# Eight of twelve modulation parts move from the start of a decoder layer into its projection stage

## The chip, the cores and the metric

The kernel runs on one core of one Trainium2 chip. The metric is device time in microseconds (us) of one execution of the whole layer; lower is better. The engines named below are PE (matrix multiply; PEld is its weight load), DVE (vector), ACT (scalar), POOL and SP. SP only issues DMA transfers here, and ACT issues a few small ones at the start.

## The reference, cut to what matters

```python
cond = silu(c)                                   # 1 x 1024
mod = cond @ ada_w[l] + ada_b[l]                 # 1024 x 6144 weights
shift1, scale1, gate1, shift2, scale2, gate2 = split(mod, 6)
h = rms_norm(x, norm_mix_w) * (1 + scale1) + shift1
mix = hybrid_mixer(h, ...)       # h @ w_in, RWKV-7, latent attention, gates, w_out
x = x + gate1 * mix
h = rms_norm(x, norm_ffn_w) * (1 + scale2) + shift2
x = x + gate2 * moe_ffn(h, ...)  # top 4 of 32 experts
```

All data are float32, with 512 tokens and 1024 features. `mod` is a single row of 6144 numbers. Of it the mixer's input needs only shift1 and scale1, which are the first 2048. The other 4096 are first used where the mixer's output is added to x.

## The kernel before

The kernel is a sequence of stages. Each is a block in which every engine has a program of its own, and engines wait for one another through counters (`wait_ge`, `then_inc`). A block ends when all engines have ended theirs.

**`phase_adaln`** makes all of `mod`. The 1024 x 6144 matrix comes as 12 chunks of 512 columns (2 MB each) through `g.ring`, which has three slots, on SP's queue. A chunk has eight groups of 128 rows. PE multiplies the first four (`PE_K`) with the condition repeated over its columns (`k{j}`, L319). DVE multiplies the other four by the condition and sums them (`accumulate`, L269), and PE adds that sum over the partitions with a matrix of ones (`p{j}`, L322). ACT copies the result (`mod{j}`, L240). A float32 matmul is two instructions in the trace. When the first four parts are there, PE turns them into columns (`mcol`, L328) and turns the normalised x (`xn`, L244) into feature-major form (`h{k}`, L336), and DVE applies scale and shift (L281) to give `hT`. Behind part 11 SP stores the other 4096 numbers in `mod_rows`.

**`phase_project`** multiplies `hT` by `w_in`. A feature block is eight matmuls (L454). The order of the first ten is l0, l1, r0 to r3, k0 to k3. ACT copies each out (`raw`, L494), and DVE mixes each with its shifted self (`shift`, L550 and L552). Behind k3 come the small products zw, za, g and ss. ACT makes sigmoids of zw and za (L506, L508) and later roots of ss (L517), while PE goes on with v and m. From the roots on DVE works through four long groups of elementwise steps (L573 to L603) and ends with L606. **`phase_rwkv`** is the recurrence.

**`phase_mla`** is the attention. Its last part goes over 32 units, eight heads for each of four blocks of 128 queries. For unit u PE issues `scores(u + 2)` (L1035, L1036), `turn(u)` (L1044) and `values(u - 1)` (L1053). DVE scales an output (L1206), takes a maximum (L1216), negates it (L1218) and inverts a sum (L1210). ACT makes the exponentials. At the start of this stage SP loads the three chunks OA, OB and GA. **`phase_output`** uses OA, OB and then GA, and reads `mod_rows` back over all partitions near its end. Routing and experts follow.

What sets the order is the hand-written program of each engine. The SP program matters most, because a wait in it also holds every transfer behind it.

## Time and profile before

| | us |
|---|---|
| median of 3 runs (1943.92 to 1948.35) | 1947.18 |
| the profiled execution | 1953.72 |
| its span in the profile | 1951.9 |
| lengths of the stages in that span: `phase_adaln` | 89.1 |
| first ten feature blocks of `phase_project` | 68.9 |
| rest of `phase_project` | 65.1 |
| the 32 units of attention, with the turn of their output | 58.2 |

Times of rows are us from the span's start. "Busy" is the time in which an engine has an instruction under way. The busy time of PE is modelled and includes its pipeline, so the distance between the starts of two PE rows says more than the length of one. "PEclk" is the granted TensorE clock as a share of full speed (1.00 is 2.4 GHz, 0.50 is 1.2 GHz).

### The profile page before, as it was taken

The numbers are of one execution on the slowest core, as the hardware profiler recorded it, in microseconds if no ns is written. First come the engines' busy times: TensorE is split into PE (matmuls) and PEld (weight loads), VectorE is DVE, ScalarE is ACT, GpSimd is POOL, SyncE is SP. The second block draws the span as 40 slices with busy tenths as digits, with TensorE's granted clock in tenths as the row PEclk, the third lists the DMA queues.
The fourth block names the chain that finished last, engine by engine and source line by source line (L and its number), as shares of the span: only waits on it lengthen the run. The fifth ranks groups of instructions, "written<-read, shape, count | busy, mean of one in ns | idle before, by whom it ended". The sixth has DMA issues, their size and how long they took to land.

```text
span 1951.9 us, 30583 instructions
## 1 busy us (share of the span) xinstructions
PE 1817.2 (93%) x11056; PEld 1401.9 (72%) x11056; DVE 1421.0 (73%) x1609; ACT 1089.9 (56%) x1175; POOL 336.2 (17%) x248
## 2 busy tenths in 40 slices
PE   5899997659999856999999999999999999999998
PEld 2444697348478854888888888888888888888884
DVE  4516743545134546999999999999999999999994
ACT  2013322345312223777777777777777777777771
POOL 3000240120000001122131221221212212212220
PEclk9999999769999966999999999999999999999998
DMA  9920000400131216999999999999999999999996
GB/s 349 346 78 0 2 4 4 156 0 1 43 129 44 87 57 235 380 370 367 365 374 369 366 364 374 365 368 365 370 368 367 367 374 368 368 373 362 374 360 239
DMA packets 247409, 500.39 MB, mean 256 GB/s; under 512 B 14730, under 2 KB 16839, under 8 KB 246131
## 3 DMA queue, kind: packets, MB, share of 16 engines
q1 hardware_dynamic: 235108, 480.87, 68.1%
q0 software_dynamic: 9648, 17.32, 2.4%
q10 hardware_dynamic: 2592, 1.31, 0.2%
q8 instruction: 47, 0.77, 0.2%
q14 instruction: 14, 0.11, 0.0%
HBM read 495.76 MB, written 21.51 MB: 265 GB/s over the span
## 4 chain that ended last, share of the span: by engine, by line
PE 60%; DVE 0%; ACT 0%; ACTq 0%; issue 0%
PE bank L1806 18%; PE bank L1804 18%; PE bank L1805 18%; PE bank L1801 2%; PE bank L1819 1%; PE bank L1791 1%; PE bank L1882 1%; PE bank L1876 1%; DVE sb_e_lo L2002 0%; ACT sb_e_hi L1888 0%; DVE sb_mod L2090 0%; DVE sb_mod L2093 0%; DVE sb_x L2095 0%; ACTq L1737 0%; DVE sb_x_lo L1999 0%; ACT sb_y L1898 0%
## 5 line engine op out<-in xcount | busy, mean ns | idle before, releaser
L2002 DVE TENSOR_TENSOR sb_e_lo<-sb_w_raw,sb_e_hi 128x2048 fp32r<-128x2048 f32 x388 | 875.6, 2284 | 1.8 <-ACT sb_e_hi L1888 1.8
L1888 ACT CAST sb_e_hi<-sb_w_raw 128x2048 fp32r<-128x2048 f32 x389 | 742.7, 1910 | 82.1 <-PE bank L1806 48.8
L1804 PE MATMUL bank<-sb_e_hi,sb_x_hi 128*128 128x512 f32 x1032 | 409.7, 397 | 0.0
L1806 PE MATMUL bank<-sb_e_hi,sb_x_lo 128*128 128x512 f32 x1032 | 404.3, 392 | 0.0
L1805 PE MATMUL bank<-sb_e_lo,sb_x_hi 128*128 128x512 f32 x1032 | 403.4, 391 | 0.0
L1973 POOL TENSOR_TENSOR sb_tick<-sb_ones 128x1 f32<-128x1 f32 x64 | 158.2, 2471 | 874.5 <-DVE sb_row L2071 697.2
L1806 PEld LDWEIGHTS bank<-sb_e_hi,sb_x_lo 128*128 128x128 f32 x1032 | 194.2, 188 | 42.6
L1805 PEld LDWEIGHTS bank<-sb_e_lo,sb_x_hi 128*128 128x128 f32 x1032 | 194.6, 189 | 40.3
L1804 PEld LDWEIGHTS bank<-sb_e_hi,sb_x_hi 128*128 128x128 f32 x1032 | 194.7, 189 | 36.6
L1804 PE MATMUL bank<-sb_e_hi,sb_a_hi 128*128 128x512 f32 x512 | 205.5, 401 | 0.0
L1806 PE MATMUL bank<-sb_e_hi,sb_a_lo 128*128 128x512 f32 x512 | 200.3, 391 | 0.0
L1805 PE MATMUL bank<-sb_e_lo,sb_a_hi 128*128 128x512 f32 x512 | 199.6, 390 | 0.0
L1806 PEld LDWEIGHTS bank<-sb_e_hi,sb_a_lo 128*128 128x128 f32 x512 | 96.1, 188 | 21.0
L1805 PEld LDWEIGHTS bank<-sb_e_lo,sb_a_hi 128*128 128x128 f32 x512 | 96.4, 188 | 18.4
L1804 PEld LDWEIGHTS bank<-sb_e_hi,sb_a_hi 128*128 128x128 f32 x512 | 96.2, 188 | 18.0
L1933 ACT ACTIVATE sb_a_hi<-bank 128x256 fp32r<-128x256 f32 x128 | 49.2, 384 | 94.8 <-PE bank L1819 90.8
L454 PE MATMUL bank<-sb_hT,sb_ring 128*128 128x512 f32 x224 | 96.5, 592 | 1.5 <-PEq L147 1.5
L2044 DVE SCALAR_TENSOR_TENSOR sb_a_lo<-bank,sb_a_hi 128x256 fp32r<-128x256 f32 x128 | 53.9, 421 | 50.3 <-ACT sb_a_hi L1933 43.9
L454 PEld LDWEIGHTS bank<-sb_hT,sb_ring 128*128 128x128 f32 x224 | 42.5, 190 | 55.4 <-issue 55.4
L1895 ACT ACTIVATE sb_mod<-bank 128x256 f32<-128x256 f32 x129 | 49.2, 382 | 49.3 <-PE bank L1806 49.2
L2009 DVE TENSOR_SCALAR sb_mod<-bank 128x256 f32<-128x256 f32 x129 | 54.2, 420 | 30.1 <-ACT sb_mod L1895 19.0
L1891 ACT CAST sb_x_hi<-bank 128x512 fp32r<-128x512 f32 x66 | 38.8, 587 | 55.9 <-PE bank L1791 55.9
(398 smaller groups left out, 2447.7 us busy)
## 6 DMA issues: line engine op xcount, KB each, us to landing
sb_w_raw<-in_w_gate_up_dram SPq DMA_DIRECT2D x262, 1024.0 KB, 6.8
sb_w_raw<-in_w_down_dram SPq DMA_DIRECT2D x128, 1024.0 KB, 7.3
sb_ring<-in_ada_w_dram SPq DMA_DIRECT2D x12, 2048.0 KB, 12.2
sb_ring<-in_w_in_dram SPq DMA_DIRECT2D x7, 2048.0 KB, 9.9
sb_x<-in_x_dram SPq DMA_DIRECT2D x2, 2048.0 KB, 12.9
sb_ring<-in_w_out_dram SPq DMA_DIRECT2D x2, 2048.0 KB, 8.0
sb_e_hi<-y_rows SPq DMA_DIRECT2D x4, 1024.0 KB, 8.5
sb_e_lo<-y_rows SPq DMA_DIRECT2D x4, 1024.0 KB, 15.7
```

The costliest lines, as they stand in the source:

```text
L454: mm = te.matmul(bank[name][:, 0:cols], lhsT, rhs, start=(n == 0), stop=(n == len(pairs) - 1))
L1801: te.matmul(out, g.bias_pick[:, :], g.bias[:, 256 * what:256 * what + 512], start=True, stop=False)
L1804: te.matmul(out, hi[:, k0 + k, :], w_hi, start=(first and k == 0 and what >= 2 * GU), stop=False)
L1805: te.matmul(out, hi[:, k0 + k, :], w_lo, start=False, stop=False)
L1806: mm = te.matmul(out, lo[:, k0 + k, :], w_hi, start=False, stop=(last and k == 3))
L1888: return sc.copy(g.e_hi[:, p % PARTS, :, :], raw(p))
L1895: return sc.activation(gated_c[:, n % 2, :], gate, ACT.Silu, scale=ALPHA)
L1933: sc.activation(g.a_hi[:, 2 * n:2 * n + 2, :], ps[bank][:, 0:2 * P].rearrange("p (k n) -> p k n", k=2), ACT.Copy, scale=1.0 / ALPHA).then_ ...
L1973: po.tensor_tensor(g.tick[:, i:i + 1], g.ones[:, 0:1], g.ones[:, 0:1], ALU.mult).then_inc(ticked, 1)
L2002: return ve.tensor_tensor(g.e_lo[:, p % PARTS, :, :], raw(p), g.e_hi[:, p % PARTS, :, :].bitcast(F32), ALU.subtract).then_inc(split_done[p ...
L2009: return ve.tensor_scalar(up_c[:, n % 2, :], ups(n), LIMIT + 1.0, 1.0 - LIMIT, ALU.min, ALU.max)
L2044: ve.scalar_tensor_tensor(g.a_lo[:, at, :], ps[bank][:, 0:2 * P].rearrange("p (k n) -> p k n", k=2), 1.0 / ALPHA, g.a_hi[:, at, :].bitcast ...
```

## The change

`phase_adaln` now makes four parts only. Three come through the ring, and the fourth has a buffer of its own, so the loads of `w_in` follow directly. Columns of shift and scale come from 16 matmuls with one output column each (L324 of the changed kernel) in place of 16 transposes. Six of the eight groups of transposes of x stand ahead of part 3, and ACT shares the last scaling with DVE.

The other eight parts are made wholly by DVE, in `phase_project`. Each is eight multiply-adds of 128 x 512 (`ad{j}{k}`), 64 in all, put behind the mixes of l0 (2), l1 (6) and each r and k (7). Their weights come as 16 halves of 1 MB into four staging slots in `g.x` and `g.mod`. Each finished sum (256 KB, still over 128 partitions) is stored in `mod_parts`, from two alternating accumulators: the first step of part j waits for the store of part j - 2 (`parts_out`). ACT's sigmoids of zw write into `g.x`, so they wait for the last of the 64.

In `phase_mla` SP loads `mod_parts` in the ring slot that GA had. PE sums each part over the partitions in one matmul (`late_sum`, before `turn(u)` for u = 2, 5, ..., 23), DVE copies each sum out (`md{j}`), POOL applies the second norm's weight, SP stores `mod_rows`, and only then loads GA.

```diff
+ADA0, LO, RKV, MLA, OA, OB, GA, GB, WOUT, N_CHUNKS = 0, 3, 4, 7, 8, 9, 10, 12, 14, 16
...
+            sp.dma_start(g.ada_last[:, :, :], ada_chunk(a, 3)).then_inc(last_in, 16)
+            for i in range(RING):
+                sp.wait_ge(*pe.at(f"k{i}"))
+                sp.wait_ge(*vec.at(f"a{i}_{KD - 1}"))
+                load_chunk(g, sp, i + RING)
...
+            for j in range(3):
+                modulation(j)
+            te.wait_ge(*act.at(f"xn{NT - 1}"))
+            for k in range(5):
+                features(k)
+            te.wait_ge(*act.at("mod2"))
+            features(5)
+            modulation(3)
+
+            te.wait_ge(*act.at("mod3"))
+            for i in range(2 * KD):
+                mm = te.matmul(ps[0][:, i:i + 1], g.mod1[0:1, i // 4, P * (i % 4):P * (i % 4) + P], g.ones[0:1, 0:1], start=True, stop=True)
+            mm.then_inc(*pe("mcol"))
+            te.wait_ge(*vec.at("h0"))
+            features(6)
+            te.wait_ge(*act.at("h1"))
+            features(7)
...
+        for name, n in (("l0", 2), ("l1", 6), *((f"{x}{i}", 7) for x in "rk" for i in f4)):
+            late_at[name] = late_ops[done:done + n]
...
+            sp.wait_ge(*vec.at("no_bias"))
+            for h in HALVES:
+                j, rows = h // 2, 512 * (h % 2)
+                if h % 2 == 0:
+                    if j >= 2:
+                        sp.wait_ge(*vec.at(f"ad{j - 2}0"))
+                    bias(j)
+                if h >= 4:
+                    sp.wait_ge(*vec.at(f"ad{j - 2}{4 * (h % 2) + 3}"))
+                sp.dma_start(staged[h % 4], ada_chunk(g.a, j + 4, rows, rows + 512)).then_inc(late_in[h % 4], 16)
+                if h >= 4 and h % 2:
+                    part(j - 2)
+                for at, chunk, last in ((5, RKV + 2, "l1"), (11, MLA, "r3")):
+                    if h == at:
+                        sp.wait_ge(*pe.at(last))
+                        load_chunk(g, sp, chunk)
+            part(LATE - 2)
+            part(LATE - 1)
...
+            sc.wait_ge(*vec.at(late_ops[-1]))
...
+                    if k % 4 == 0:
+                        h = 2 * j + k // 4
+                        ve.wait_ge(late_in[h % 4], 16 * (h // 4 + 1))
+                    if k:
+                        ve.wait_ge(*vec.at(f"ad{j}{k - 1}"))
+                        before = acc
+                    else:
+                        ve.wait_ge(bias_in[j % 2], 16 * (j // 2 + 1))
+                        if j >= 2:
+                            ve.wait_ge(g.parts_out[j % 2], 16 * (j // 2))
+                    ve.scalar_tensor_tensor(acc, staged[(2 * j + k // 4) % 4][:, k % 4, :], g.cond[:, k:k + 1], before, ALU.mult, ALU.add).then_inc(*vec(n))
...
+            sp.dma_start(parts, g.mod_parts.rearrange("j p n -> p j n")).then_inc(parts_in, 16)
+            sp.dma_start(ffn_row, g.a["norm_ffn_w"]).then_inc(ffn_in, 16)
+            sp.wait_ge(*pool.at("g2"))
+            sp.dma_start(g.mod_rows, mod_row).then_inc(g.mod_out, 16)
+            sp.wait_ge(g.mod_out, 16)
+            load_chunk(g, sp, GA)
...
+                te.matmul(ps[7][0:1, :], g.ones[:, 0:1], parts[:, j, :], start=True, stop=True).then_inc(*pe(f"md{j}"))
```

Where instructions stand now, at three places. First PE at the end of `phase_adaln`, from part 3 on. Before, eight more parts come between part 3 and the end (`sb_mod` under L328 is the copied parts, `sb_xn` the normalised x):

```order
L319 MATMUL bank<-sb_ring,sb_rep 128x512 x4
L322 MATMUL bank<-sb_ada_sum,sb_ones 128x512
L328 MATMUL bank<-sb_ident,sb_mod 128x128 x16
L319 MATMUL bank<-sb_ring,sb_rep 128x512 x4
L322 MATMUL bank<-sb_ada_sum,sb_ones 128x512
L336 MATMUL bank<-sb_ident,sb_xn 128x128 x32
L319 MATMUL bank<-sb_ring,sb_rep 128x512 x4
L322 MATMUL bank<-sb_ada_sum,sb_ones 128x512
```

The same place in the changed kernel, from the transposes of x on:

```order
L310 MATMUL bank<-sb_ident,sb_xn 128x128 x24
L303 MATMUL bank<-sb_ada_last,sb_rep 128x512 x4
L306 MATMUL bank<-sb_ada_sum,sb_ones 128x512
L324 MATMUL bank<-sb_ones,sb_mod 128x1 x16
L310 MATMUL bank<-sb_ident,sb_xn 128x128 x8
L153 UNCONDITIONAL_BRANCH
L469 UNCONDITIONAL_BRANCH
L477 MATMUL bank<-sb_hT,sb_ring 128x512 x80
```

24 of 32 transposes now stand ahead of part 3, and the feature blocks (L477) follow eight transposes behind the columns. Second, DVE in `phase_project` at k2, k3 and the steps behind them, before:

```order
L550 TENSOR_SCALAR sb_lerp<-sb_raw,sb_cols 128x512
L552 SCALAR_TENSOR_TENSOR sb_Kt<-sb_raw,sb_not_mu,sb_lerp 128x512
L550 TENSOR_SCALAR sb_lerp<-sb_raw,sb_cols 128x512
L552 SCALAR_TENSOR_TENSOR sb_Kt<-sb_raw,sb_not_mu,sb_lerp 128x512
L563 TENSOR_SCALAR sb_Bt<-sb_Kt,sb_cols 128x512 x4
```

and in the changed kernel (L586 is a step of the late sums, with its weights in `sb_x` or `sb_mod`):

```order
L592 TENSOR_SCALAR sb_lerp<-sb_raw,sb_cols 128x512
L594 SCALAR_TENSOR_TENSOR sb_Kt<-sb_raw,sb_not_mu,sb_lerp 128x512
L586 SCALAR_TENSOR_TENSOR sb_v<-sb_x,sb_cond,sb_v 128x512 x6
L586 SCALAR_TENSOR_TENSOR sb_v<-sb_mod,sb_cond,sb_v 128x512
L592 TENSOR_SCALAR sb_lerp<-sb_raw,sb_cols 128x512
L594 SCALAR_TENSOR_TENSOR sb_Kt<-sb_raw,sb_not_mu,sb_lerp 128x512
L586 SCALAR_TENSOR_TENSOR sb_v<-sb_mod,sb_cond,sb_v 128x512 x7
L606 TENSOR_SCALAR sb_Bt<-sb_Kt,sb_cols 128x512 x4
```

Seven steps have come behind every mix, the last mix too, where k3 was followed at once by the steps on `sb_Bt`. Third, PE in the attention around unit 23 of the changed kernel:

```order
L1092 MATMUL bank<-sb_mod,sb_x 128x384
L1093 MATMUL bank<-sb_causal,sb_ident 128x128
L1101 MATMUL bank<-sb_ident,sb_qk 128x128 x3
L1110 MATMUL bank<-sb_v_tok,sb_probT 128x64 x3
L1092 MATMUL bank<-sb_mod,sb_x 128x384
L1093 MATMUL bank<-sb_causal,sb_ident 128x128
L1119 MATMUL bank<-sb_ring,sb_ones 1x512
```

L1119 is the only new row; without it the order of the other PE instructions of this loop is that of before. It stands between the scores of a later unit and the turn of this one.

## Rows read from the trace of the kernel before

**Rows 1.** Windows by stage: length, busy of each engine (instructions), PEclk, DMA share, GB/s.

```profile
0.00:89.10 89.10, 63.00 (x169) 29.08 (x170) 47.10 (x72) 18.63 (x28) 19.39 (x77) 0.96 0.99 355
89.10:158.00 68.90, 68.88 (x162) 30.35 (x162) 11.33 (x20) 9.10 (x13) 0.00 (x0) 1.00 0.26 89
158.00:223.10 65.10, 63.99 (x172) 30.26 (x171) 56.87 (x78) 24.69 (x43) 0.00 (x0) 1.00 0.00 0
433.80:492.00 58.20, 56.05 (x385) 48.78 (x385) 29.29 (x128) 33.52 (x102) 0.00 (x0) 0.96 0.00 1
```

**Rows 2.** Timeline of `phase_adaln`: start, length, engine, line, instruction, [idle before, releaser].

```profile
34.27 4.27 ACT L244 ACTIVATE sb_xn<-sb_x,sb_rstd 128x1024 f32<-128x1024 f32 x4 [1.41 <-DVE sb_rstd L288]
36.45 0.75 DVE L269 SCALAR_TENSOR_TENSOR sb_ada_sum<-sb_ring,sb_cond,sb_ada_b_rows 128x512 f32<-128x512 f32 x1 [2.22 <-DMA sb_ring<-in_ada_w_dram]
...
37.24 2.33 DVE L269 SCALAR_TENSOR_TENSOR sb_ada_sum<-sb_ring,sb_cond,sb_ada_sum 128x512 f32<-128x512 f32 x3
...
37.50 3.60 PE L319 MATMUL bank<-sb_ring,sb_rep 128*128 128x512 f32 x8
...
40.94 1.02 PE L322 MATMUL bank<-sb_ada_sum,sb_ones 128*128 128x512 f32 x2
...
41.99 0.58 ACT L240 COPY sb_mod<-bank 128x512 f32<-128x512 f32 x1 [2.99 <-PE bank L322]
...
50.32 0.36 DVE L277 COPY sb_mod_cols<-bank 128x4 f32<-128x4 f32 x4
...
52.31 1.91 PE L336 MATMUL bank<-sb_ident,sb_xn 128*128 128x128 f32 x16
...
55.75 2.96 DVE L281 TENSOR_SCALAR sb_hT<-bank,sb_gain,sb_mod_cols 128x512 f32<-128x512 f32 x4
...
87.69 0.58 ACT L240 COPY sb_mod<-bank 128x512 f32<-128x512 f32 x1 [4.84 <-PE bank L322]
...
89.12 8.39 PE L454 MATMUL bank<-sb_hT,sb_ring 128*128 128x512 f32 x19 [1.48 <-PEq L147]
```

**Rows 3.** Windows within `phase_adaln`, columns as in rows 1; PE had been idle since 25.2.

```profile
28.00:30.00 2.00, 0.00 (x0) 0.00 (x0) 0.00 (x0) 1.97 (x3) 0.00 (x0) 0.60 1.05 385
30.00:34.00 4.00, 2.95 (x4) 1.41 (x5) 2.86 (x4) 2.83 (x6) 0.00 (x0) 0.50 1.06 389
34.00:36.00 2.00, 2.00 (x4) 0.83 (x4) 0.23 (x2) 1.73 (x2) 0.00 (x0) 0.69 1.04 383
```

**Rows 4.** Timeline of `phase_project`: the mix of k3, the sigmoids and roots, the stage's end.

```profile
151.82 0.49 DVE L550 TENSOR_SCALAR sb_lerp<-sb_raw,sb_cols 128x512 f32<-128x512 f32 x1 [5.59 <-ACT sb_raw L494]
...
158.68 0.49 DVE L550 TENSOR_SCALAR sb_lerp<-sb_raw,sb_cols 128x512 f32<-128x512 f32 x1 [5.59 <-ACT sb_raw L494]
159.12 0.69 ACT L506 ACTIVATE sb_x<-bank,sb_cols 128x512 f32<-128x512 f32 x1 [0.47 <-PE bank L454]
159.21 0.75 DVE L552 SCALAR_TENSOR_TENSOR sb_Kt<-sb_raw,sb_not_mu,sb_lerp 128x512 f32<-128x512 f32 x1
...
169.79 0.43 DVE L580 TENSOR_SCALAR sb_rn<-sb_AR 128x512 f32<-128x512 f32 x1 [5.93 <-ACT sb_AR L517]
...
220.29 2.48 DVE L606 TENSOR_TENSOR sb_bv<-bank,sb_v 128x512 f32<-128x512 f32 x4
```

**Rows 5.** DMA issues: KB each, median us from issue to landing.

```profile
sb_w_raw<-in_w_gate_up_dram SPq DMA_DIRECT2D x262, 1024.0 KB, 6.8
sb_ring<-in_w_out_dram SPq DMA_DIRECT2D x2, 2048.0 KB, 8.0
h_rows<-sb_w_raw SPq DMA_DIRECT2D x4, 512.0 KB, 2.6
```

**Rows 6.** Attention: two starts of scores on PE one unit apart, and small matmuls.

```profile
476.70 1.08 PE L1035 MATMUL bank<-sb_mod,sb_x 96*128 96x512 f32 x2
...
478.27 1.00 PE L1053 MATMUL bank<-sb_v_tok,sb_probT 128*128 128x64 f32 x8
...
479.11 1.08 PE L1035 MATMUL bank<-sb_mod,sb_x 96*128 96x512 f32 x2
```

More of the change, by code:

```diff
@@ L112, in ring_chunks @@
     slab = MLA_IN
-    chunks = [rows(a["ada_w"], 512 * j, 512 * j + 512) for j in range(12)]
+    chunks = [ada_chunk(a, j) for j in range(RING)]
     chunks += [rows(a["w_in"], slab + 3 * WIDTH, slab + SLAB)]
@@ L141 @@
 PE_K = 4
+LATE = 8
 def phase_adaln(nc, g):
@@ L161, in phase_adaln @@
[L161 to L164 removed]
+        accs, js, ks = range(PE_K, KD), range(4), range(KD)
@@ L165, in phase_adaln, with weights, loaded @@
         ps = g.ps
         block = ctx.enter_context(nc.Block())
+        bank_of = (4, 5, 6, 7, 2, 3, 4, 5)
         unused = g.hT[:, 0:2, :].rearrange("p a n -> p (a n)")
+        def weights(j):
+            return slot(g, j) if j < RING else g.ada_last[:, :, :]
+        def loaded(j):
+            return chunk_loaded(g, j) if j < RING else (last_in, 16)
         @block.sync
@@ L318, in _ @@
                 for k in range(PE_K):
-                    mm = te.matmul(out, g.rep[:, k, :], slot(g, j)[:, k, :], start=(k == 0), stop=False)
+                    mm = te.matmul(out, g.rep[:, k, :], weights(j)[:, k, :], start=(k == 0), stop=False)
                 mm.then_inc(*pe(f"k{j}"))
@@ L958, in phase_mla @@
         prob = g.qk[:, 0, :, :].rearrange("p h n -> p (h n)").rearrange("p (a n) -> p a n", n=SEQ)
-        w_in = g.sem(ctx, "mla_weights_in")
+        w_in, parts_in, ffn_in = (g.sem(ctx, n) for n in ("mla_weights_in", "parts_in", "ffn_in"))
+        parts = slot(g, GA)
+        mod_row = parts[0:1, :, :].rearrange("p (a b) n -> p a (b n)", a=4)
+        ffn_row = g.oT[0:1, 0:2, :].rearrange("p a n -> p (a n)")
+        late_after = {3 * j + 2: j for j in range(LATE)}
         ts, units = range(NT), range(NT * HEADS)
```

197 lines of the change are left out of this document (101 added, 96 removed).

## The prediction

> **What bounds the kernel now.** I read the table of stages first [rows 1]. In the first 89.1 us the DMA engines are busy for 0.99 of the time at 355 GB/s, while PE works 63.0 and DVE 47.1 us. So this stage is a transfer: twelve chunks of weights and x. In the next 68.9 us PE is busy for 68.88, DVE for only 11.3 and the DMA engines for 0.26: ten feature blocks run back to back on PE. In the 65.1 us behind them DVE is busy for 56.9. In the attention PE is busy for 56.1 of 58.2 us. The change carries eight chunks and DVE's part of them from the first of these stretches to the second, where both resources are nearly idle, and it puts eight small sums in the attention, where PE is not idle.
>
> The timeline of the first stage says how early its end can come [rows 2]. The weights of part 3 land at 36.45, when DVE starts on them. The last part is copied out at 87.69 + 0.58 = 88.27, and the first feature block starts 0.85 later at 89.12. Everything between is parts 4 to 11, with the making of `hT` in their midst.
>
> **1. The first stage ends early.** Up to part 3 the queue carries the same bytes in the same order, so I keep 36.45. ACT has x normalised at 34.27 + 4.27 = 38.54, and PE now waits for that ahead of part 3. Then, all by [rows 2]: 24 transposes at 1.91 / 16 = 0.12 make 2.9 (41.4); the four matmuls of part 3 take 40.94 - 37.50 = 3.4 (44.9); the sum over partitions until ACT can start takes 41.99 - 40.94 = 1.05, and ACT's copy 0.58 (46.5). DVE's share of part 3, from 36.45 for 0.75 + 2.33 with a short gap, ends at 39.6, ahead of all this. The 16 one-column matmuls are 32 instructions, each with a weight load. No row has this shape. The nearest is the eight value matmuls in 1.00 us, 0.125 each [rows 6], so 4.0 (50.5). Two tiny DVE steps by the four in 0.36 take 0.4 with the hand-over (50.9). DVE's four scalings take 2.96, as four did before, and ACT does its four beside them (53.9). The last two groups of transposes hide behind the first scalings. With 0.85 for the end of the block the first feature block starts at 54.7 in place of 89.12: **-34.4 us**.
>
> The bounds of this term: one pass per column would take 2.0 off. If a weight load could not be hidden, a column would cost as much as a pass of a wide matmul, 3.4 / 8 = 0.43 [rows 2], and 32 of these would cost 13.8, or 9.8 more. The loads of `w_in` for l0 and l1 (1 MB) follow part 3 at once, 2.7 us at 389 GB/s [rows 3], so they are there by 40.
>
> **2. TensorE's clock.** After PE had been idle since 25.2, the granted clock fell from 1.00 to 0.50 (1.2 GHz) in the window from 28 to 30 and came back within that from 34 to 36, some 4 us after PE's work had started again at 31 [rows 3]. In the changed kernel PE has little to stream from 46 to 54.7: one-column matmuls, two groups of transposes, and gaps. If the clock falls there, the first 4 us of feature blocks run at half speed and lose about 2, and half of the columns cost double, another 2. If it doesn't, nothing is lost. I take **+1.5**, with 0 and 4 as ends.
> The Trainium skill ("TensorE: Matmul & The Clock Gate", section "What's actually happening") says that the low clock is the default state and activity releases it. By that rule the columns would not hold the clock up and I would have to take the upper end, 4. The trace before has no stretch that decides whether such thin matmuls count.
>
> **3. DVE sums eight parts beside PE.** A step of 128 x 512 has a distance of 0.78 (three in 2.33) [rows 2]. Feature blocks come every 158.68 - 151.82 = 6.86 us [rows 4]. One mix takes 159.21 + 0.75 - 158.68 = 1.28, and seven steps take 5.5, together 6.8. DVE just keeps up, with 0.1 us to spare per block. All 64 steps are 50 us, of which 43 to 44 lie beside PE's feature blocks. The last seven do not: they follow k3's mix, which follows PE's last block.
>
> The cost is read behind k3 [rows 4]. The mix ended at 159.96 and ACT's first sigmoid had started at 159.12. It now waits for the last step, 159.96 + 5.5 = 165.4 on the old time scale, so it starts 6.3 later. Queued behind it on ACT are the other seven sigmoids, the squares, the copies of g and the roots. PE's g waits for the bank of the first sigmoid. DVE's L580 waits for the roots, until 169.79 before and 176.1 now. From L580 on DVE works nearly without a gap to the stage's end (L606, 220.29 + 2.48), so nothing takes the delay back: **+6.3**.
>
> Then the waits within. Each half is loaded into a slot that was freed three halves, about 13 us, before it is needed (a half is used up every 68.6 / 16 = 4.3 us), and a 1 MB load lands in 6.8 even in a full queue [rows 5]. That is hidden. The stores are tighter. Part j's first step waits for the store of part j - 2, with eight steps and a mix or two in between, 7.5 us. The store stands behind a half (2.7 us of data) and moves 0.26 MB (0.7 us); a 0.5 MB store takes 2.6 from issue to landing [rows 5]. So it lands 5.5 to 6 us after its issue, and fits. Two stores are issued closely behind loads of `w_in` (2 MB, 5.4 us; 1.7 MB, 4.4 us) in the same queue. Counted from PE's first block, with DVE's first mix 7.8 later: step 8 is done at 20.7, a half, the store of part 0, the 2 MB, two halves and the store of part 1 then keep the queue from 22.2 to 37.1 (2.7 + 0.7 + 5.4 + 5.4 + 0.7), so that store lands at about 37.8, and part 3's first step is due at 38.1. For part 6 the same count from step 32 at 45.8 gives 61.9 against 61.1, 0.8 late. I take **+0.7**; none is the lower end, and 4 the upper, if every landing behind such a load is 2 us later, as one store's whole 2.6.
> The Trainium skill ("DMA: Bandwidth & Descriptors", section "Anatomy of one DMA") has a rule that speaks against this step: most of a transfer's fixed 2.0 us is the wait until the last byte is confirmed, and that is longest where the target is HBM. The store of 2.6 agrees with the size of it. With one more such 2.0 us at the two tight places the waits would come to about 4.
>
> **4. The sums in the attention.** PE gives 1.05 us per sum (two passes until the next engine can start), with a distance of two passes, 0.86 [rows 2]; the output has one partition, but 512 columns stream as before. PE's busy share here is 0.96 [rows 1], and two starts of scores lie 2.41 us apart [rows 6], so a pass in this queue costs its own length: 8 x 0.86 = 6.9. DVE's eight copies (0.74 each, as a scaling) mostly fit in its idle time (29.3 busy of 58.2 us), but in the short units of the first query block they can hold the next maximum back: 0.6 in all. **+7.5**. Ends: 3.5 if half of it falls into waits of PE for ACT; 6.9 + 8 x 0.74 = 12.8 if each copy is on the chain too. POOL's two products and the late load of GA (8.0 us for 2 MB [rows 5]) start behind unit 24 and have eight units of 2.41 us and the whole of OA's and OB's products to hide in; without that cover GA would cost its 8.0.
>
> **The sum.** -34.4 + 1.5 + 6.3 + 0.7 + 7.5 = -18.4 us. From the profiled execution's 1953.7 that gives 1935.3. That execution was 6.5 above the median of the three runs, and I lay the same difference on the median: 1947.2 - 18.4 = **1929** (1928.8). All later stages start from counters and not at fixed times, so they shift as a whole. What cannot be told from no change is 0.2%, 3.9 us.
>
> **Rivals.**
> - *DVE falls behind PE.* The waits for stores and halves are not 0.7 but 4 us, the columns cost 5 more, and the clock 4. For it speaks that a block leaves 0.1 us to recover in. Against it speaks the low DMA share of that stretch. The sum is -34.4 + 5 + 4 + 6.3 + 4 + 7.5 = -7.6: 1940.
> - *More is hidden.* The last steps are covered by slack in ACT's queue, or the sums by PE's waits, 3 to 4 us each: -18.4 - 7 = -25.4, 1922. Against it speak PE's 0.96 and DVE's 56.9 of 65.1 us.
> - *It ends slower.* The halves' round trip, SP's program in order with a wait for DVE, a load and a store in each turn, exceeds the 13 us that a slot has. Each of the 12 reloads would then hold DVE, and PE behind it through `raw`'s four buffers. To pass the point at which the gain of 18.4 is gone plus 3.9, a reload must be late by 22.3 / 12 = 1.9 us, that is, land 14.9 us after its slot is free. With 3 us late it is 12 x 3 - 18.4 = +18: 1965. Against it: the 6.8 us of [rows 5].
> - *It doesn't do what it says.* The first stage is not shorter because something other than the chunks holds its end, or a later stage gives the time back: 1947. Against it: POOL's constants are 19.4 us of work [rows 1], x is normalised at 38.5, and no later wait is on a transfer issued in the first stage.
>
> **How the numbers follow.** The forecast gets 0.66, more hidden 0.12, DVE behind 0.12, slower 0.05, no effect 0.05. With the bounds of the four terms combined as mostly independent, the likeliest case reaches from 1923 to 1936. More hidden and the better half of DVE behind widen that to **1920 to 1939**, which leaves out about 2 in 10. Faster by over 0.2%: 0.66 + 0.12 + 0.12 = 0.90; within: 0.04; slower: 0.06.
>
> **What would show it.** Step 1: the first L477 row at 54.7, with the busy time of L324 near 4. Step 2: PEclk at 0.5 or 1.0 in the windows from 46 to 60. Step 3: L586 rows at 0.78, no DMA named as their releaser but at parts 3 and 6, the last of them some 7 us behind PE's last k block; from there to the next stage 65.1 + 7. Step 4: 58.2 + 7.5 us from the first score to the end of that stage. The prediction is wrong if the first feature block starts beyond 60, if DMA releases many L586 rows, or if the expert stages change their length.

## The result, and the profile after

The changed kernel takes 1937.04 us, median of five runs (1934.9 to 1942.24), beside 1948.35 for the kernel before in the same series. The ratio is 0.9949, 95% interval 0.9929 to 0.9968. In a second series the same two gave 1938.46 and 1948.43, ratio 0.9957 (0.9941 to 0.9972). So it is faster by 10 to 11 us, where 18.4 were forecast. One of the six executions of the kernel with filler (experiment 11) took 3683.56 us; its ratio leaves that execution out, and what slowed it stays open. All landmarks below are from profiled executions: 1953.72 us before, 1942.24 after, 11.5 apart.

| landmark, us | before | after | gain so far |
|---|---|---|---|
| first feature block | 89.12 | 56.52 | 32.60 |
| PE's last k block done | 157.96 | 127.92 | 30.04 |
| ACT's first sigmoid | 159.12 | 138.01 | 21.11 |
| RWKV's stage starts | 223.09 | 202.60 | 20.49 |
| first score of the attention | 433.79 | 412.58 | 21.21 |
| end of the attention | 491.99 | 479.43 | 12.56 |
| end of the span | 1951.9 | 1940.5 | 11.4 |

The windows by stage, with the columns of [rows 1]:

```profile
0.00:56.50 56.50, 32.79 (x105) 18.93 (x106) 19.21 (x32) 16.84 (x24) 19.05 (x77) 0.89 0.83 293
56.50:127.90 71.40, 71.38 (x160) 31.23 (x160) 50.41 (x74) 9.10 (x13) 0.00 (x0) 0.96 0.86 311
127.90:202.60 74.70, 66.43 (x169) 31.23 (x169) 65.56 (x90) 24.69 (x43) 0.00 (x0) 0.95 0.02 8
412.60:479.40 66.80, 64.49 (x400) 49.49 (x400) 34.32 (x136) 34.34 (x101) 4.68 (x2) 0.97 0.10 33
```

Against [rows 1], DVE's work has moved from the first line to the second (11.3 to 50.4 us), and each of the three later stretches has grown: 68.9 to 71.4, 65.1 to 74.7, 58.2 to 66.8. The mean granted clock of the second and third is now 0.96 and 0.95, where both had 1.00 before.

The timeline of `phase_adaln`, as [rows 2]:

```profile
36.53 0.75 DVE L270 SCALAR_TENSOR_TENSOR sb_ada_sum<-sb_ada_last,sb_cond,sb_ada_b_rows 128x512 f32<-128x512 f32 x1 [2.24 <-DMA sb_ada_last<-in_ada_w_dram]
...
38.65 2.84 PE L310 MATMUL bank<-sb_ident,sb_xn 128*128 128x128 f32 x24 [1.37 <-ACT sb_xn L240]
41.33 3.60 PE L303 MATMUL bank<-sb_ada_last,sb_rep 128*128 128x512 f32 x8
...
45.82 0.58 ACT L234 COPY sb_mod<-bank 128x512 f32<-128x512 f32 x1 [6.76 <-PE bank L306]
46.46 5.58 PE L324 MATMUL bank<-sb_ones,sb_mod 1*128 1x1 f32 x32 [0.68 <-ACT sb_mod L234]
...
52.56 2.96 DVE L287 TENSOR_SCALAR sb_hT<-bank,sb_gain,sb_mod_cols 128x512 f32<-128x512 f32 x4
53.42 1.97 PE L310 MATMUL bank<-sb_ident,sb_xn 128*128 128x128 f32 x8 [1.38 <-DVE sb_hT L287]
...
56.52 1.19 PE L477 MATMUL bank<-sb_hT,sb_ring 128*128 128x512 f32 x1 [1.12 <-PEq L153]
```

Up to ACT's copy the forecast is met within 0.1 us (46.40 against 46.5). Then the 32 one-column matmuls take 5.58 and not 4.0. The windows say why, and also why eight transposes at 53.42 take 1.97 where eight of the 24 at 38.65 took 0.95:

```profile
46.00:48.00 2.00, 1.54 (x14) 1.54 (x14) 0.00 (x0) 0.41 (x1) 0.00 (x0) 1.00 1.06 389
48.00:50.00 2.00, 2.00 (x12) 2.00 (x11) 0.00 (x0) 0.00 (x0) 0.00 (x0) 0.51 0.69 250
50.00:60.00 10.00, 7.49 (x22) 5.02 (x23) 4.40 (x9) 2.89 (x4) 0.00 (x0) 0.50 0.07 9
60.00:62.00 2.00, 2.00 (x4) 0.86 (x3) 0.00 (x0) 0.00 (x0) 0.00 (x0) 0.58 1.00 375
```

The granted clock falls from 1.00 to 0.50 (1.2 GHz) at 48, in the midst of the one-column matmuls, and is back at 1.00 only at about 61.7, some 5 us after the feature blocks have begun.

The end of `phase_project`'s first half, as [rows 4]: the three first steps that waited for a store (parts 3, 5 and 6), the last mix, the last seven steps, and what waited for them.

```profile
97.40 3.97 DVE L586 SCALAR_TENSOR_TENSOR sb_v<-sb_mod,sb_cond,sb_v 128x512 f32<-128x512 f32 x5 [0.37 <-DMA mod_parts<-sb_v]
...
113.09 2.33 DVE L586 SCALAR_TENSOR_TENSOR sb_v<-sb_mod,sb_cond,sb_v 128x512 f32<-128x512 f32 x3 [0.76 <-DMA mod_parts<-sb_v]
...
123.29 1.54 DVE L586 SCALAR_TENSOR_TENSOR sb_v<-sb_x,sb_cond,sb_v 128x512 f32<-128x512 f32 x2 [2.81 <-DMA mod_parts<-sb_v]
...
131.77 0.75 DVE L594 SCALAR_TENSOR_TENSOR sb_Kt<-sb_raw,sb_not_mu,sb_lerp 128x512 f32<-128x512 f32 x1
132.44 5.54 DVE L586 SCALAR_TENSOR_TENSOR sb_v<-sb_mod,sb_cond,sb_v 128x512 f32<-128x512 f32 x7
138.01 0.69 ACT L530 ACTIVATE sb_x<-bank,sb_cols 128x512 f32<-128x512 f32 x1 [9.40 <-DVE sb_v L586]
```

PE's last k block is done at 127.92, and the sigmoid starts 10.09 later; before it was 1.16. The last mix ends 4.60 behind PE's last block (132.52), before 2.00: DVE had lost 3.9 us to the stores, and 2.6 of them were still there. The DMA issues of this stretch, as [rows 5]:

```profile
sb_x<-in_ada_w_dram SPq DMA_DIRECT2D x8, 1024.0 KB, 7.1
sb_mod<-in_ada_w_dram SPq DMA_DIRECT2D x8, 1024.0 KB, 8.5
mod_parts<-sb_v SPq DMA_DIRECT2D x8, 256.0 KB, 7.2
```

and DMA's busy share from 56 to 142 us, in 40 slices of 2.15 us, in tenths:

```profile
DMA  0499998000999999999999969999999970030030
```

The halves land in 7 to 8.5 us by the median, near the 6.8 assumed (12.0 at the longest). A store of 256 KB takes 7.2 by the median, where the forecast had 5.5 to 6. The one that held part 6 took 10.4.

The end of the stage shows one more delay. From the sigmoid to RWKV's start it is 64.59 us, before 63.97. DVE's steps keep their distances down to the last four, the bonus products (L651, before L606), and the last two of these now wait for PE:

```profile
200.74 0.69 DVE L651 TENSOR_TENSOR sb_bv<-bank,sb_v 128x512 f32<-128x512 f32 x1 [0.17 <-PE bank L477]
201.59 0.69 DVE L651 TENSOR_TENSOR sb_bv<-bank,sb_v 128x512 f32<-128x512 f32 x1 [0.17 <-PE bank L477]
```

PE had stood idle for 7.2 us behind k3 and then worked for some 5 us at a granted clock of 0.50, so it was behind DVE at the end.

In the attention each sum takes two passes on PE in 1.02, then DVE's copy of one row.

```profile
455.12 1.02 PE L1119 MATMUL bank<-sb_ring,sb_ones 128*1 128x512 f32 x2
456.18 0.68 DVE L1296 COPY sb_ring<-bank 1x512 f32<-1x512 f32 x1 [0.95 <-PE bank L1119]
```

### The profile page after: what moved, and what is told of

The parts are those of the page before. It is cut to its first block, busy times and chain, and to the rows that moved or that the text cites. A ratio compares the mean times of both kernels' runs of the same rounds, so it can differ in the third digit from the quotient of the medians.

```text
span 1940.5 us, 30529 instructions
## 1 busy us (share of the span) xinstructions
PE 1800.6 (93%) x11008; PEld 1395.9 (72%) x11008; DVE 1445.8 (75%) x1642; ACT 1089.0 (56%) x1171; POOL 342.3 (18%) x250
## 3 DMA queue, kind: packets, MB, share of 16 engines
q1 hardware_dynamic: 237430, 485.07, 68.9%
## 4 chain that ended last, share of the span: by engine, by line
PE 60%; DMA 0%; DVE 0%; ACT 0%; issue 0%; ACTq 0%; POOLq 0%
PE bank L1882 18%; PE bank L1880 18%; PE bank L1881 18%; PE bank L1877 2%; PE bank L1895 1%; PE bank L1867 1%; PE bank L1958 1%; DMA sb_e_hi<-y_rows 0%; DMA y_rows<-sb_y,sb_goal_now 0%; DVE sb_e_lo L2078 0%; ACT sb_e_hi L1964 0%; DVE sb_mod L2166 0%; DVE sb_mod L2169 0%; DVE sb_x L2171 0%; ACTq L1813 0%
## 5 line engine op out<-in xcount | busy, mean ns | idle before, releaser
L2049 POOL TENSOR_TENSOR sb_tick<-sb_ones 128x1 f32<-128x1 f32 x64 | 169.2, 2644 | 873.4 <-DVE sb_row L2147 697.2
L1881 PEld LDWEIGHTS bank<-sb_e_lo,sb_a_hi 128*128 128x128 f32 x512 | 96.4, 188 | 18.4
L477 PE MATMUL bank<-sb_hT,sb_ring 128*128 128x512 f32 x224 | 99.1, 605 | 1.1 <-PEq L153 1.1
L477 PEld LDWEIGHTS bank<-sb_hT,sb_ring 128*128 128x128 f32 x224 | 43.4, 194 | 56.2 <-issue 56.2
```

What stands on the lines that cost most here:

```text
L477: mm = te.matmul(bank[name][:, 0:cols], lhsT, rhs, start=(n == 0), stop=(n == len(pairs) - 1))
L1881: te.matmul(out, hi[:, k0 + k, :], w_lo, start=False, stop=False)
L2049: po.tensor_tensor(g.tick[:, i:i + 1], g.ones[:, 0:1], g.ones[:, 0:1], ALU.mult).then_inc(ticked, 1)
```

## The experiments

Each kernel starts from the changed one, unless it says otherwise, and is called by its number below. Small differences are read from landmarks of the profile rather than from whole times: the stretch from RWKV's start to the first score varied from 204.2 to 210.1 us in kernels that were alike in it.

**1. The columns by transposes**

```
-    mm = te.matmul(ps[0][:, i:i + 1], g.mod1[0:1, i // 4, P * (i % 4):P * (i % 4) + P], g.ones[0:1, 0:1], ...)
+    mm = te.transpose(ps[0][:, i:i + P], g.mod1[:, i // 4, P * (i % 4):P * (i % 4) + P], g.ident[:, :])
```

> The 16 pairs of one-column matmuls (L324, 5.58 us) are replaced by 16 overlapping 128-column transposes that leave the same 16 columns. Theory (thin columns stream next to nothing, so TensorE's clock falls during them): the 16 transposes take about 1.9 us, PEclk stays at 1.00 from 46 to 64, the first feature block starts at about 52.3 (56.52 less 3.7 for the columns and 0.5 for the two late transposes), and the first raw copy follows it by 7.8 instead of 9.7. The end of the kernel comes 4 to 7 us earlier than in the changed kernel: about 1931 to 1933 by the median. Rival (the clock falls because PE waits for ACT and DVE in this stretch, whatever shape the columns have): PEclk still falls to 0.50 near 50, the first raw copy stays 9.7 behind the first block, and only the 2 to 4 us of the columns are gained: about 1934.

Measured: 1931.08 us, ratio to the kernel before 0.9918 (0.9901 to 0.9934).

```profile
46.40 1.97 PE L324 MATMUL bank<-sb_ident,sb_mod 128*128 128x128 f32 x16 [0.68 <-ACT sb_mod L234]
...
59.31 0.59 ACT L517 COPY sb_raw<-bank 128x512 f32<-128x512 f32 x1 [7.64 <-PE bank L477]
```

```profile
50.00:52.00 2.00, 0.84 (x8) 0.60 (x6) 1.85 (x3) 1.67 (x3) 0.00 (x0) 1.00 0.00 0
52.00:64.00 12.00, 11.83 (x28) 5.40 (x29) 3.75 (x7) 0.59 (x1) 0.00 (x0) 1.00 0.77 279
```

The first feature block came at 52.17, the clock stayed at 1.00, and the first raw copy followed by 7.14 instead of 9.70. So the fallen clock and the columns cost 4.4 us ahead of the first block and 2.6 behind it. The rival failed here. Whether it was the shape of the transposes that held the clock is another question; 2, 3, 4 and the combined kernel (10) bear on it.

**2. 128 columns through one row**

```
-    ..., g.mod1[0:1, ...], g.ones[0:1, 0:1], ...      # out ps[0][:, i:i + 1]
+    ..., g.mod1[0:1, ...], g.ones[0:1, 0:P], ...      # out ps[0][:, i:i + P]
```

> The same 16 one-row matmuls as in the changed kernel, but each streams 128 columns of ones instead of one, so the number of instructions stays 32 and only what each streams grows. Theory (streamed columns hold the clock): PEclk stays near 1.00 until 52, and the 32 instructions cost 32 x 0.12 = 3.8 us or less at the full clock, no more than the 5.58 of the thin ones; the first raw copy follows the first block by 8 or less. Rival (a matmul with only one row of weights counts for little whatever it streams, or the waits decide): PEclk falls to 0.50 within 46 to 54 as before and the 32 instructions cost 5.6 or more.

Measured: 1935.95 us, 0.9943 (0.9926 to 0.9959). The clock fell during the 32 instructions, about 2.7 us after their start at 47.99, and the first raw copy came 9.01 behind the first block:

```profile
48.00:50.00 2.00, 2.00 (x18) 2.00 (x19) 0.00 (x0) 0.00 (x0) 0.00 (x0) 1.00 0.74 275
50.00:52.00 2.00, 2.00 (x15) 2.00 (x14) 0.00 (x0) 0.00 (x0) 0.00 (x0) 0.68 0.08 32
```

PE is busy for the whole of both windows, and the clock falls in the second. The 32 took 4.73, between the two forecasts. Streaming more columns through one row didn't hold the clock.

**3. One column through 128 rows**

```
+    mm = te.matmul(ps[0][:, i:i + 1], g.mod1[:, i // 4, ...], g.ident[:, 0:1], ...)
```

> The columns again by matmuls that stream one column, but with all 128 rows of the weights in use (the rows of the modulation are alike, and the moving column is the first of the identity), where the changed kernel has one row. The first pair of runs showed that streaming 128 columns through one row leaves the clock falling (it was down to 0.68 in 50 to 52), which spoke against my idea that the thin stream lets it fall. Theory (what counts is how much of the array the matmuls use; one row is next to nothing): PEclk stays at 1.00 through the 32 instructions, they cost 32 x 0.125 = 4.0 or less, the first feature block comes at about 54 and the first raw copy 7.2 behind it; the kernel is 4 to 5 us faster than the changed one: 1932.5. Rival (short matmuls with a weight load each let the clock fall, however many rows they use; then only transposes, which are half as many and stream 128, hold it): PEclk 0.50 from about 50, first raw copy 9 or more behind the first block, 1936 to 1937.

Measured: 1940.59 us, 0.9949 (0.9929 to 0.9969). The 32 instructions took 3.73, all at the full clock, but it fell as they ended (0.68 in 50 to 52, 0.50 until 60), and the first raw copy came 9.96 behind the first block. The time lies above both forecasts (1932.5, 1936 to 1937): the stretch from RWKV's start to the first score, which the edit doesn't touch, was at its long end, 210.1 us. The theory about rows fell like the one about columns.

**4. 128 columns through 128 rows**

```
+    mm = te.matmul(ps[0][:, i:i + P], g.mod1[:, i // 4, ...], g.ident[:, :], ...)
```

> The columns by 16 ordinary matmuls with all 128 rows of the weights in use and 128 columns streamed, 32 passes: both of the properties together that the two earlier kernels had one at a time (128 columns through one row; one column through 128 rows), and in both of those the clock was down from about 50.7. Theory (both rows and columns must be full to hold the clock): PEclk stays at 1.00 to 64, the 32 passes take 3.6 to 3.8 us, first raw copy 7.2 to 7.8 behind the first block. Rival (even full matmuls can't, because the transposes held the clock only by being done 2 us after they started; what lets it fall is the gap between the last wide matmul of part 3 and the first block, now 2 us longer): PEclk 0.50 somewhere from 52 to 58, the first raw copy 9 or more behind the first block.

Measured: 1935.42 us, 0.9938 (0.9919 to 0.9957). The 32 passes took 3.84. The clock held through them and fell behind them; the first raw copy was 8.54 behind the first block:

```profile
50.00:52.00 2.00, 1.85 (x17) 1.66 (x15) 0.04 (x1) 0.00 (x0) 0.00 (x0) 1.00 0.06 24
52.00:54.00 2.00, 0.77 (x7) 0.77 (x8) 1.93 (x5) 1.63 (x3) 0.00 (x0) 1.00 0.00 0
54.00:56.00 2.00, 0.67 (x4) 0.46 (x3) 1.52 (x5) 1.16 (x2) 0.00 (x0) 0.77 0.00 0
56.00:58.00 2.00, 2.00 (x3) 0.80 (x3) 0.90 (x1) 0.00 (x0) 0.00 (x0) 0.50 0.00 1
```

The fall came not in the columns but in PE's waits between them and the first block, where PE was busy for 0.77 and 0.67 of 2 us. That fits the rival. It doesn't come every time, though: kernel 1 had such waits too (0.61 of 2 us busy from 48 to 50, 0.84 from 50 to 52) and kept its clock.

**5. Without the sums in the attention** (the rows for the second norm are then not computed)

```
-    late_after = {3 * j + 2: j for j in range(LATE)}
+    late_after = {}
...
-    po.wait_ge(*vec.at(f"md{LATE - 1}"))
+    po.wait_ge(parts_in, 16)
+    po.wait_ge(*vec.at("rs23"))
```

> The eight late sums on PE and their eight copies on DVE are left out of the attention (the rows written for the second norm are then wrong; what is timed is the rest). Theory (each sum costs its two passes on PE plus about 0.2 of copying and hand-over): the stretch from the first score to the end of the attention falls from 66.9 to about 58.2, the whole kernel is 8.6 us faster than the changed one, 1928.4. Rival (the 8.65 us in this stretch come partly from something else that moved there, POOL's products or the loads of the parts and of GA): only 3 to 7 us come back.

Measured: 1928.71 us, 0.9905 (0.9889 to 0.9922). From the first score to the end of the attention it took 58.08 us:

```profile
408.90:467.00 58.10, 55.87 (x384) 48.61 (x385) 29.28 (x128) 33.53 (x102) 4.68 (x2) 0.97 0.11 38
```

POOL's two products (4.68 us) and the loads still stood in the attention, and it had its old length. The 8.65 us are the sums and their copies alone; the clock began the attention at 0.50 in this profile as in the changed kernel's, so the two compare (see step 4 below).

**6. Without the last seven steps** (the last part is then incomplete)

```
-    sp.wait_ge(*vec.at(f"ad{j}{KD - 1}"))
+    sp.wait_ge(*vec.at(f"ad{j}{KD - 1 if j < LATE - 1 else 0}"))
...
+    late_ops = late_ops[:-7]
+    late_at["k3"] = []
```

> The last seven of the 64 steps on DVE, behind k3's mix, are left out (the last part is then incomplete). Theory (ACT's first sigmoid, and everything behind it, waits for these steps alone): 5.5 us of steps disappear, the sigmoid starts about 3.5 behind PE's last k block instead of 10.1 (DVE then still lags by the 3.9 us that it waited for stores), and the whole kernel is 5.5 us faster than the changed one, 1931.5. Rival (most of the delay is DVE's backlog from waiting for the stores and from its late start): the sigmoid starts earlier by the same 5.5, but RWKV's stage begins only 2 to 4 us earlier, since the squares and roots wait for something else.

Measured: 1929.17 us, 0.9909 (0.9891 to 0.9928). The sigmoid started 3.08 behind PE's last k block, 7.0 sooner than in the changed kernel, and RWKV's stage 67.1 behind it instead of 74.7. That is 1.5 more than the steps themselves: with the seven gone the last step lies ahead of k3's mix, and the sigmoid no longer waits for the mix either (1.2). The rival failed, since RWKV's stage moved by all of it and 0.6 more: PE no longer stood idle for 7 us, the clock stayed at 1.00, and from the sigmoid to RWKV's start it was 63.98 again.

**7. Four accumulators instead of two**

```
-    late_acc, bias_row = g.v[:, 0:2, :], g.v[:, 2:4, :]
+    late_acc, bias_row = [g.v[:, 0, :], g.v[:, 1, :], g.late_more[:, 0, :], g.late_more[:, 1, :]], g.v[:, 2:4, :]
...
-    if j >= 2:
-        ve.wait_ge(g.parts_out[j % 2], 16 * (j // 2))
+    if j >= 4:
+        ve.wait_ge(g.parts_out[j % 4], 16)
```

> The late sums go round four accumulators instead of two, so that part j waits for the store of part j - 4 and not of part j - 2. Theory (DVE lost 3.9 us in three waits for stores, and these add to the tail behind k3): no L586 row is released by a store, the first sigmoid starts about 6.5 to 7 behind PE's last k block instead of 10.1, and the kernel is 3 to 3.5 us faster than the changed one: about 1933.7. Rival (the stores were late because the queue is full, and the halves behind them are as late): DVE waits for halves in their place, and at most 1 us is won.

Measured: 1935.94 us, 0.9937 (0.992 to 0.9953). No step waited for a DMA.

```profile
127.22 0.75 DVE L594 SCALAR_TENSOR_TENSOR sb_Kt<-sb_raw,sb_not_mu,sb_lerp 128x512 f32<-128x512 f32 x1
127.89 5.54 DVE L586 SCALAR_TENSOR_TENSOR sb_late_more<-sb_mod,sb_cond,sb_late_more 128x512 f32<-128x512 f32 x7
...
133.46 0.69 ACT L530 ACTIVATE sb_x<-bank,sb_cols 128x512 f32<-128x512 f32 x1 [6.80 <-DVE sb_late_more L586]
```

PE's last k block ended at 125.97, so the mix ended 2.00 behind it, as before the change, and the sigmoid came 7.49 behind it: 6.33 more than before, which is the forecast's +6.3 for the tail. The stores' waits were thus worth 2.6 us at the sigmoid. From the sigmoid to RWKV's start it is 63.98 again (before 63.97, changed 64.59), but this 0.6 doesn't go with the waits: among the kernels that kept them the stretch is 64.0 (kernel 4) to 65.1 (kernel 9), and the whole difference arises where DVE's last steps wait for PE. Halves that are as late, the rival, didn't show.

**8. The steps begun earlier**

```
-    for name, n in (("l0", 2), ("l1", 6), *((f"{x}{i}", 7) for x in "rk" for i in f4)):
+    for name, n in (("pre", 4), ("l0", 4), ("l1", 7), *((f"{x}{i}", 7) for x in "rk" for i in range(3 if x == "k" else 4)), ("k3", 0)):
```

> All 64 steps are kept, but begin earlier: four ahead of l0's mix, where DVE was idle, four behind l0, seven behind each other mix, and none behind k3's. Theory (the first sigmoid waits for the seven steps behind k3's mix, 5.5 us, and for DVE's backlog of stores, 3.9): the tail goes, the waits for stores stay, so the sigmoid starts 4 to 5 behind PE's last k block instead of 10.1, and the kernel is about 5.5 us faster than the changed one: 1931.5. Rival (what is moved forward only waits for its halves, whose landing the queue sets): DMA releases more L586 rows, the sigmoid stays 8 to 10 behind k3, and the kernel is within 2 us of the changed one.

Measured: 1930.41 us, 0.9902 (0.9875 to 0.9928). The sigmoid started 1.51 behind PE's last k block, better than theory and rival had it. One step was still held by a store (1.51 us, the first of part 6), and k3's mix ended 2.66 behind PE's last block, but nothing of the late sums lay behind it any more. All 64 steps now lie beside PE's blocks, and RWKV's stage starts 65.5 behind the last k block (before 65.1).

**9. The sums in the MLA stage**

```
+    for j in range(LATE):
+        mm = te.matmul(ps[7][0:LATE, :], g.pick[:, 7 - j:15 - j], parts[:, j, :], start=(j == 0), stop=(j == LATE - 1))
```

`pick` is zero but for a column of ones, so sum j lands in row j of one bank; two steps on DVE apply norm_ffn_w to the eight rows.

> The eight late sums leave the attention: the parts are loaded at the start of the MLA stage, PE sums them into the eight rows of one bank in eight matmuls behind its second group of up-projections, where it waited 8.23 us for DVE, and DVE makes the eight rows of modulation in two steps while POOL works. Nothing is left out. Theory (in the attention each sum costs its passes because PE is full there, in the MLA stage it would be free because PE waits): from the first score to the end of the attention 58.2 instead of 66.9, the first score where it was, the kernel 8 us faster than the changed one: about 1929. Rival (the sums, the 2 MB load of the parts ahead of OA and OB, or DVE's two steps land on the path of the MLA stage): the first score comes 3 to 6 us later, and only 2 to 5 us are won: 1932 to 1935.

Measured: 1929.73 us, 0.9896 (0.9875 to 0.9916). In the MLA stage the sums lie in PE's wait, and the first score comes 57.82 behind the stage's first transposes (58.62 in the changed kernel):

```profile
365.05 7.03 PE L1084 MATMUL bank<-sb_ring,sb_pick 128*8 128x512 f32 x16
375.78 3.09 PE L1093 MATMUL bank<-sb_ident,sb_qk 128*96 128x128 f32 x16 [3.69 <-DVE sb_qk L1278]
```

The attention took 57.91. The same 16 passes that cost 8.65 us where PE was the bound show no cost here, but it isn't nothing for certain. PE's wait ahead of the turn went from 8.23 to 3.69 us with 7.03 us of passes put in, and the turn came 23.2 us behind the stage's start, against 22.9, while the mean granted clock up to the first score rose from 0.70 to 0.80. In the two combined kernels (10 and 11), which have these sums too, the stretch took 59.9 and 59.8 us, against 55.3 to 59.1 in those without.

**10. All four together** (1, 7, 8 and 9), with nothing left out

> The changed kernel with four edits together, nothing left out: the columns by 16 transposes, four accumulators, the 64 steps begun four earlier with none behind k3, and the sums in the MLA stage. Theory (the prices add, since they lie at three places in a row): first feature block at 52.2, the first sigmoid 1.2 to 1.6 behind PE's last k block (itself at about 121), RWKV's stage from about 187.5 (202.60 less 6.9 and 8.5), 58 from the first score to the end of the attention instead of 66.9; against the changed kernel 6.9 + 8.5 + 8.9, at most 24, earlier: about 1913 to 1916. Rival (with PE at full clock from the start, DVE can no longer keep up, and the queue, which has 16 halves and three chunks to carry from 54 on, becomes the bound of the ten blocks): DMA releases L586 rows, the sigmoid stays 4 or more behind k3, and the time is 1918 to 1921.

Measured: 1917.55 us (1915.79 to 1918.34), 0.9847 (0.983 to 0.9863), 21 us below the changed kernel on the same chip. The time missed the forecast of 1913 to 1916 by 1.5 us. The first block at 52.12, the sigmoid 1.22 behind PE's last k block and RWKV's stage from 187.84 came about as added up; the attention took 56.69 where 58 were expected, because it began at the full clock (see step 4 below), and the MLA stage 1 us more than in the changed kernel. PE's last k block ended at 122.66 and not at 121, because the clock fell this time, although the columns were transposes:

```profile
48.00:52.00 4.00, 1.41 (x11) 0.94 (x9) 3.31 (x6) 2.78 (x4) 0.00 (x0) 1.00 0.26 97
52.00:54.00 2.00, 1.88 (x3) 0.97 (x4) 1.09 (x3) 0.00 (x0) 0.00 (x0) 0.64 0.03 8
54.00:56.00 2.00, 2.00 (x3) 0.67 (x2) 0.00 (x0) 0.00 (x0) 0.00 (x0) 0.50 0.49 94
```

The rival (the queue as the bound) failed: no step but the first half's waited for a DMA.

**11. The same with filler on PE.** Starts from the combined kernel.

```
+    def keep_busy(n):
+        for _ in range(n):
+            te.matmul(ps[1][:, :], g.ones[:, :], g.mod1[:, 3, :], start=True, stop=True)
...
+    keep_busy(3)        # ahead of the wait for h0
...
+    keep_busy(3)        # behind features(7)
```

> The combined kernel, plus six matmuls of 512 columns and full rows whose result nobody reads: three behind the transposes of the columns, while PE waits for DVE's first scaling, and three behind the last transposes of xn, while PE waits for the next part of the program. They are 12 passes of 0.215, 1.3 us at each place, about as long as PE was idle there (1.38 and 1.33), so they should delay nothing. In the combined kernel the clock fell behind the transposes (0.64 in 52 to 54, 0.50 in 54 to 56), in the first kernel with transposes it did not, and with full matmuls it fell behind them (0.77 in 54 to 56): the shape of the columns did not decide it. Theory (PE's idle time and the thin work between part 3 and the first block let the clock fall, whatever the columns look like): PEclk 1.00 in all windows from 46 to 64, the first raw copy 7.1 behind the first block instead of 8.8, RWKV's stage starts 1 to 2 us earlier than 187.84, the kernel is 1 to 2 us faster than 1917.5. Rival (the fall has another cause, such as the length of full use before it): the clock falls in spite of the filler, and the time is 1917 to 1919.

Measured: 1916.56 us, 0.9839 (0.9826 to 0.9852), which the intervals don't tell from the combined kernel.

```profile
48.49 2.74 PE L315 MATMUL bank<-sb_mod,sb_ones 128*128 128x512 f32 x6
...
55.01 13.54 PE L483 MATMUL bank<-sb_hT,sb_ring 128*128 128x512 f32 x31 [0.33 <-PEq L153]
...
62.16 0.59 ACT L523 COPY sb_raw<-bank 128x512 f32<-128x512 f32 x1 [9.23 <-PE bank L483]
```

```profile
46.00:56.00 10.00, 8.99 (x40) 5.27 (x40) 4.26 (x9) 3.48 (x5) 0.00 (x0) 1.00 0.32 119
56.00:64.00 8.00, 8.00 (x20) 3.56 (x19) 2.41 (x4) 0.59 (x1) 0.00 (x0) 1.00 0.77 279
```

With PE busy for 8.99 of the 10 us the clock stayed at 1.00 and the first raw copy came 7.15 behind the first block. One profile of each can't show that the filler held it, since kernel 1 had kept the clock without any. The filler was sized wrongly: a pass of 512 columns is 0.43 and not 0.215, so each group took 2.74 us and the first block came 2.9 later, which cost more than the clock gave (RWKV's stage from 189.02, not 187.84).

**12. The changed kernel again**

> The changed kernel itself once more, beside the kernel before and the combined kernel on one chip, since differences of 1 to 3 us between kernels of different chips can't be read otherwise. Expected: 0.9949 of the kernel before, within 0.002; first block at 55 to 57, first sigmoid 9.2 to 10.1 behind PE's last k block, 65.4 to 66.9 from the first score to the end of the attention, as every kernel with these parts unchanged showed so far. A ratio beyond 0.9925 or 0.9970 would mean that the first measurement was off.

Measured: the second series named above, 1938.46 us, 0.9957. First block at 55.01, the one-column matmuls in 3.73, the first raw copy 8.80 behind the first block, the sigmoid 9.67 behind the last k block, 66.90 in the attention. The clock fell at about 51.5 this time (mean 0.88 in 50 to 52), behind the columns, so the same code lost 2.8 us less than in the first profile.

## Why the prediction was right or wrong

The direction and the stages were right, and so was each mechanism that was named; three of the sizes were not. The measured 1937 to 1938 lies near the upper end of the range (1920 to 1939), and nearer to the rival in which DVE falls behind PE (1940: clock 4, waits 4, columns 5 more) than to the forecast of 1929. Of that rival the dear clock came true and the waits in part; its columns didn't. The gain was put 7.0 too high in the profiled executions (-11.4 against -18.4). By the steps:

| step | forecast | measured | shown by |
|---|---|---|---|
| 1, the first stage, at full clock | -34.4 | -35.2 | 1 |
| 2, the clock | +1.5 | +5.1 | 1 |
| 3, the tail | +6.3 | +6.3 | 7, 8 |
| 3, waits for stores | +0.7 | +2.6 | 7 |
| 3, the clock behind k3 | 0 | +0.6 | rows of L651 |
| 4, the sums | +7.5 | +8.65 | 5, 9 |
| elsewhere | 0 | +0.5 | |

- **Step 1** held. At the full clock the columns take 3.73, by the nearest small matmuls I had 4.0. With that and transposes at 0.12 the first block would stand at 52.17 + 3.73 - 1.97 = 53.93, against the forecast's 54.7.
- **Step 2** was mis-sized, and it is half of the error. Counted from the start of the columns to the first raw copy, 14.67 us would do (kernel 1's 12.91, with 3.73 in place of 1.97 for the columns). Seven profiles with the columns unchanged (six kernels, the changed one twice) took 17.0 to 19.8, 2.3 to 5.1 more, on average 3.9; the first profile was among the dearest. The sum had 1.5, as though a fall were as likely as none, and the clock fell in all seven. The Trainium skill ("TensorE: Matmul & The Clock Gate", "What's actually happening"), by which the low clock is the default and activity releases it, had pointed to the upper end, 4; the seven profiles agree with it.
- **Step 3's tail** was exact: 6.33 with four accumulators. **Its waits** were mis-sized: the places were right (parts 3 and 6, and 5 beside them), but the store of part 4, which part 6 waits for, landed later than the count of the queue had it. In kernel 1, where the clock stayed up, part 6's first step was due 61.0 us behind PE's first block (counted 61.1), and the store landed at 63.4 (counted 61.9). In the changed kernel the store landed 10.4 us after its issue, behind the 1.7 MB load for MLA and two halves. The row of DMA's busy share above has idle slices from 71 to 77, when all four slots were full, and then 47 us in which all slices but one are at 9: there was no slack in the queue to take a delay back. Which part of the count was off stays open. The three waits were 3.9 us in all, and 2.6 of them were still there at k3's mix. The Trainium skill's extra time for a confirmed write ("DMA: Bandwidth & Descriptors", "Anatomy of one DMA", given there for transfers that GpSimd issues) had given about 4 for these waits, near the 3.9 by luck: in the full queue each store of the changed kernel landed 0.64 to 0.67 us behind the half ahead of it, about the time that its 256 KB take, so no extra time for confirmation shows. The last two stores, in an idle queue, landed 2.0 us after their issue.
- **The clock behind k3** was a term put at nothing. PE stood idle for 7.2 us between its products of zw and za and those of g, the granted clock fell to 0.50 and was back some 5 us after PE had started again, and PE, which before the change had been ahead of DVE to the end, made DVE's last steps wait. In eight profiles with this idle stretch and the two accumulators it cost 0.05 to 1.15 us.
- **Step 4** was right in mechanism and 1.15 low: the copies and hand-overs cost 0.22 a sum beyond the two passes of 0.86, where 0.08 was assumed. The attention comes in two lengths, and the granted clock of its first 4 us tells which:

```profile
433.80:437.80 4.00, 4.00 (x19) 4.00 (x20) 1.48 (x8) 2.88 (x8) 0.00 (x0) 0.50 0.00 0
412.60:416.60 4.00, 4.00 (x19) 4.00 (x20) 1.47 (x8) 2.87 (x8) 0.00 (x0) 0.50 0.00 0
401.10:405.10 4.00, 3.81 (x26) 2.90 (x26) 2.14 (x12) 3.31 (x11) 0.00 (x0) 1.00 0.00 0
398.00:402.00 4.00, 3.81 (x31) 3.59 (x31) 2.41 (x14) 3.31 (x11) 0.00 (x0) 1.00 0.01 2
```

These are the kernel before, the changed one, kernel 8 and the combined one. Of nine profiles with the sums, the five that begin at 0.50 took 66.8 to 66.9 and the four that begin at 1.00 took 65.4. Without the sums it is 57.9 to 58.2 at 0.50 (before, kernels 5 and 9) and 56.7 at 1.00 (10 and 11). So the sums cost 8.7 us at either level, and a late clock adds 1.5 of its own.
- **Elsewhere**: RWKV and MLA together were 0.7 shorter, everything behind the attention 1.2 longer. In the kernels with the sums in the attention the part behind it was 1460.8 to 1461.1, in those without 1459.7 to 1460.3. What makes this 0.5 to 1.2 us stays open; it wasn't tried.

Of the signs named in advance, 54.7 was missed by the clock, the releasers at parts 3 and 6 and the attention's 58.2 + 7.5 came true but for a part 5 and 1.15 us, and the expert stages kept their length but for 0.8 us.

## What to carry to other kernels

When work is moved from a stage that waits for transfers to a stage with an idle engine, price the seam: here the first stage gave its 35 us, and 8.9 us of DVE's tail and waits, 8.7 us of sums in a full PE, and 2 to 5 us of clock took two thirds back. Most of it, 21 of 24 us, could be had back without touching the idea (kernel 10): by writing the columns as transposes, by starting the moved steps where DVE idled, by giving the stores two more buffers, and by putting eight small sums where PE waited. Here a store shared one queue with loads that were issued as early as their slots allowed, and it took up to 10.4 us where 2.0 did in the idle queue: give such stores slack, in buffers, for the loads that can stand ahead of them.
